# A two-layer transformer block on one core: the sums over channels added on VectorE before one product with ones, and the convolution's steps spread differently over the attention's rounds

## The reference

```python
def rms_norm_2(x, g):                       # over the 1024 channels
    y = xf * lax.rsqrt(jnp.mean(xf * xf, axis=-1, keepdims=True) + NORM_EPS)
    return (y * g).astype(x.dtype)

def layer_norm(x, g, b):
    mu = jnp.mean(xf, axis=-1, keepdims=True)
    xc = xf - mu
    y = xc * lax.rsqrt(jnp.mean(xc * xc, axis=-1, keepdims=True) + NORM_EPS)
    ...
for l in range(DEPTH_2):
    n = rms_norm_2(h, mix_norm_g[l])
    proj = jnp.einsum("btd,de->bte", n, w_in[l])     # q, k, v, indexer, rnn, conv, gates
    attn = dsa_attention(...)                        # top-64 keys per query, 8 heads
    rnn = rg_lru_branch(...)
    cnv = conformer_conv_branch(...)                 # 31-tap depthwise conv, layer_norm, swish
    h = h + (g_attn * attn @ w_o_attn + g_rnn * rnn @ w_o_rnn + g_conv * cnv @ w_o_conv) @ w_out
    f = rms_norm_2(h, ffn_norm_g[l])
    h = h + (silu(f @ w_gate) * (f @ w_up)) @ w_down
return h[:, N_META:]
```

## Time and profile before

| | |
|---|---|
| median of 3 runs | 1950.4 us (1950.38 to 1953.06) |
| profiled execution, its own time | 1948.66 us |
| its span, first to last instruction | 1946.9 us |
| mean granted TensorE clock | 0.996 |
| PE busy | 1885.7 us (97% of the span) |
| PEld busy | 1494.1 us (77%) |
| DVE busy | 735.4 us (38%) |
| ACT busy | 479.4 us (25%) |
| POOL busy | 98.4 us (5%) |
| HBM read | 222.34 MB, 115 GB/s over the span |

### The profile page before, as it was taken

How to read it: one execution, slowest core, us unless ns; L and a number is a source line. 1 busy time by engine, 2 the same in 40 slices (tenths; PEclk the granted TensorE clock), 3 DMA queues, 4 the chain that set the end, 5 groups by cost and what they waited for, 6 DMA issues and landing times.

```text
span 1946.9 us, 31281 instructions
## 1 busy us (share of the span) xinstructions
PE 1885.7 (97%) x13612; PEld 1494.1 (77%) x13612; DVE 735.4 (38%) x1518; ACT 479.4 (25%) x1012; POOL 98.4 (5%) x117
## 2 busy tenths in 40 slices
PE   8999999888889999999999999999999999999999
PEld 3344645888878888788888888887887888888888
DVE  1234426555533876754221000027859442210000
ACT  2112235333334114552202000041135422010000
POOL 0001300323300000000000000000000000000000
PEclk9999999999999999999999999999999999999999
DMA  8311300000043343332333433433433333433442
GB/s 312 140 58 67 114 22 2 4 4 4 4 154 130 130 151 130 130 128 90 120 140 109 156 147 151 143 139 130 152 130 130 130 108 130 151 130 141 162 161 99
DMA packets 33225, 225.41 MB, mean 116 GB/s; under 512 B 4672, under 2 KB 6080, under 8 KB 6336
## 3 DMA queue, kind: packets, MB, share of 16 engines
q1 hardware_dynamic: 33088, 223.40, 32.1%
HBM read 222.34 MB, written 1.05 MB: 115 GB/s over the span
## 4 chain that ended last, share of the span: by engine, by line
PE 89%; DVE 5%; issue 2%; DVEq 1%; ACT 1%; SPq 1%; DMA 0%; POOL 0%; ACTq 0%
PE PS L450 22%; PE PS L596 12%; PE PS L1554 8%; PE PS L615 8%; PE PS L621 8%; PE PS L634 8%; PE PS L1192 2%; PE PS L463 1%; PE PS L1493 1%; PE PS L1194 1%; DVE arena L840 1%; PE PS L1169 1%; PE PS L1645 1%; PE PS L569 1%; DVEq L842 1%
## 5 line engine op out<-in xcount | busy, mean ns | idle before, releaser
L450 PE MATMUL PS<-arena,ring 128*128 128x272 f32 (+1 forms) x2176 | 499.7, 390 | 0.0
L450 PEld LDWEIGHTS PS<-arena,ring 128*128 128x128 f32 x2176 | 413.0, 191 | 77.1 <-issue 1.4
L596 PE MATMUL PS<-arena,ring 128*128 128x272 f32 (+1 forms) x1024 | 229.6, 386 | 2.1 <-DVE arena L1036 2.1
L596 PEld LDWEIGHTS PS<-arena,ring 128*128 128x128 f32 x1024 | 194.5, 190 | 35.8 <-DVE arena L1036 2.9
L840 DVE SCALAR_TENSOR_TENSOR arena<-arena,par 128x272 f32<-128x272 f32 (+1 forms) x480 | 214.9, 489 | 16.3 <-issue 0.4
L615 PE MATMUL PS<-arena,ring 128*128 128x272 f32 (+1 forms) x704 | 163.8, 386 | 0.0
L621 PE MATMUL PS<-arena,ring 128*128 128x272 f32 (+1 forms) x704 | 163.8, 386 | 0.0
L1554 PE MATMUL PS<-arena,ring 128*128 128x512 f32 (+2 forms) x448 | 158.3, 514 | 1.7 <-DVEq L1845 1.7
L634 PE MATMUL PS<-arena,ring 128*128 128x272 f32 (+1 forms) x704 | 157.1, 386 | 1.1 <-issue 1.1
L634 PEld LDWEIGHTS PS<-arena,ring 128*128 128x128 f32 x704 | 133.8, 190 | 24.5 <-issue 1.9
L615 PEld LDWEIGHTS PS<-arena,ring 128*128 128x128 f32 x704 | 133.9, 190 | 22.7
(11 more groups left out here) (327 smaller groups left out, 1918.5 us busy)
## 6 DMA issues: line engine op xcount, KB each, us to landing
ring<-stream_dram SPq DMA_DIRECT2D x207, 1024.0 KB, 4.9
arena<-x_dram SPq DMA_DIRECT2D x1, 2048.0 KB, 11.6
cst<-const_dram SPq DMA_DIRECT2D x1, 1080.0 KB, 7.2
out_dram<-H SPq DMA_DIRECT2D x4, 256.0 KB, 2.2
cst<-const_dram SPq DMA_DIRECT2D x1, 912.0 KB, 17.6
arena<-stream_dram SPq DMA_DIRECT2D x1, 512.0 KB, 7.2
par<-param_dram SPq DMA_DIRECT2D x2, 177.0 KB, 11.0
c<-const_dram SPq DMA_DIRECT2D x1, 128.0 KB, 2.5
```

Source lines behind the costliest of these rows:

```text
L450: last = mm(PS[:, (m + f) % 4, nw], lslot(l, n, KD, 256)[:, k, P * f:P * f + P], NT[:, k, nw], start=k == 0, stop=k == KD - 1)
L596: last = mm(PS[:, i % 4, NQ], lslot(l, n, KD, 256)[:, k, P * (i % 2):P * (i % 2) + P], src[:, k, NQ], start=k == 0, stop=k == KD - 1)
```

## The change

Three things are changed.

1. A sum over channels is made in two parts: VectorE adds the 8 channel groups to one (`add_tiles`, a `tensor_reduce` whose innermost axis is the group, so that it steps 272 elements between reads), and TensorE does one product of `ones` with the result (`sum_parts`). There are 9 such places: 5 in layer 0, 4 in layer 1. New semaphores (`added`, `fn_added`, `conv_sq_in`) carry it, and each place has a new target (`SQF`, `SQS`, `CSUM`).
2. The order around the sums: in layer 0 the mix norm's sum stands behind the second indexer projection in place of the first; the feed-forward norm's sum stands behind the first gate tile in place of the first up tile; VectorE makes `H` behind `MIX` in place of ahead of it, and ScalarE waits for it (`h_made`) before it keeps the projections.
3. `conv_until` has other numbers.

```diff
+        CSUM = TQ[:, 1:3, :]
-            def sum_tiles(src, bank, n, done):
-                for k in range(n):
-                    last = mm(PS[:, bank, NQ], ones, src[:, k, NQ], start=k == 0, stop=k == n - 1)
-                last.then_inc(done, 1)
+            def sum_parts(src, bank, nw, done):
+
+                mm(PS[:, bank, nw], ones, src[:, nw], start=True, stop=True).then_inc(done, 1)

             def norm_sums(nth, bank, nw):

-                for k in range(KD):
-                    pe.wait_ge(L["sq"], B["sq"] + KD * nth + k + 1)
-                    last = mm(PS[:, bank, nw], ones, SQ2[:, k, nw], start=k == 0, stop=k == KD - 1)
-                last.then_inc(L["sums"], 1)
+                pe.wait_ge(L["added"], B["added"] + nth + 1)
+                sum_parts(SQS, bank, nw, L["sums"])
...
                 if m == 0 and l == 0:
-                    pe.wait_ge(fn_sq, KD)
-                    for k in range(KD):
-                        last = mm(PS[:, 4, META:T2], ones, SQ1[:, k, 0:TX], start=k == 0, stop=k == KD - 1)
-                    last.then_inc(fn_sums, 1)
-                if m == 0:
+                    pe.wait_ge(fn_added, 1)
+                    sum_parts(SQF, 4, slice(META, T2), fn_sums)
+                if m == (0 if l else 1):
                     norm_sums(0, 5, NW)
...
                     pe.wait_ge(L["conv_sum_in"], B["conv_sum_in"] + 1)
-                    sum_tiles(CVG, 4, KD, L["conv_sum"])
+                    sum_parts(CSUM[:, 0], 4, NQ, L["conv_sum"])
                 if i == 8:
-                    pe.wait_ge(L["conv_sq"], B["conv_sq"] + 1)
-                    sum_tiles(CSQ, 5, KD, L["conv_sq_sum"])
+                    pe.wait_ge(L["conv_sq_in"], B["conv_sq_in"] + 1)
+                    sum_parts(CSUM[:, 1], 5, NQ, L["conv_sq_sum"])
...
                 last.then_inc(L["gate_made"], 1)
+                if i == 0:
+                    norm_sums(1, 4, NQ)
...
                 last.then_inc(L["up_made"], 1)
-                if i == 0:
-                    norm_sums(1, 4, NQ)
...
                 inverse_root(RS2[:, 0, :], MIX, D, L["root"])
+                act.wait_ge(h_made, 1)
...
+        def add_tiles(v, out, tiles):
+
+            return v.tensor_reduce(out, tiles.rearrange("p k t -> p t k"), axis=AX_X, op=ALU.add)
...
+            if l == 0:
+                dve.wait_ge(fn_sq, KD)
+                add_tiles(v, SQF[:, META:T2], SQ1[:, :, 0:TX]).then_inc(fn_added, 1)
+            dve.wait_ge(L["sq"], B["sq"] + KD)
+            add_tiles(v, SQS, SQ2).then_inc(L["added"], 1)
             dve.wait_ge(L["lam_exp"], B["lam_exp"] + 1)
...
                 dve.wait_ge(fn_root, 1)
-                for k in range(KD):
-                    stt(H[:, k, META:T2], XT[:, k, TX:T1], final_g[:, k:k + 1], RSF[:, META:T2], ALU.mult, ALU.mult)
                 dve.wait_ge(L["sums"], B["sums"] + 1)
...
                 tt(MIX[:, META:T2], MIX[:, META:T2], RSF[:, META:T2], ALU.mult).then_inc(mix_in, 1)
+                for k in range(KD):
+                    last = stt(H[:, k, META:T2], XT[:, k, TX:T1], final_g[:, k:k + 1], RSF[:, META:T2],
+                               ALU.mult, ALU.mult)
+                last.then_inc(h_made, 1)
...
-            conv_until = (68, 90, 94, 96, 98, 98, 106, 124) if len(R) == 6 else (68, 90, 100, 102, 104, 124)
+            conv_until = (68, 80, 86, 90, 92, 94, 106, 124) if len(R) == 6 else (68, 80, 88, 92, 98, 124)
...
-            dve.sem_inc(L["conv_sum_in"], 1)
+            add_tiles(v, CSUM[:, 0, NQ], CVG[:, :, NQ]).then_inc(L["conv_sum_in"], 1)
...
+                if i == 6:
+                    dve.wait_ge(L["conv_sq"], B["conv_sq"] + 1)
+                    add_tiles(v, CSUM[:, 1, NQ], CSQ[:, :, NQ]).then_inc(L["conv_sq_in"], 1)
...
-            dr()
+            dve.wait_ge(L["sq"], B["sq"] + 2 * KD)
+            add_tiles(v, SQS[:, NQ], SQ2[:, :, NQ]).then_inc(L["added"], 1)
             dve.wait_ge(L["root"], B["root"] + 2)
```

More of the change, by code:

```diff
@@ L242, in build @@
         DEC = cut(7024, KD, T2)
-        RSF, MIX, COSR, SINR = (RS2[:, i, :] for i in range(1, 5))
+        RSF, MIX, COSR, SINR, SQS, SQF = (RS2[:, i, :] for i in range(1, 7))
         MG = RG
@@ L279, in build @@
         steps_over, vt_made, vt_kept = sem("steps_over"), sem("vt_made"), sem("vt_kept")
-        zeroed = [sem(f"zeroed{i}") for i in range(60)]
+        zeroed = [sem(f"zeroed{i}") for i in range(64)]
         SCAN_COUNTS = dict(
@@ L357, in build @@
         KSQ, RSK = cut(30136, 2, T2), cut(30680, 2, T2)
-        consts2_in, params2_in, fm_ready, mix_in = sem("consts2_in"), sem("params2_in"), sem("fm_ready"), sem("mix_in")
+        consts2_in, params2_in, fm_ready, fn_added, mix_in, h_made = (
+            sem("consts2_in"), sem("params2_in"), sem("fm_ready"), sem("fn_added"), sem("mix_in"), sem("h_made"))
         out_in = sem("out_in")
         LAYER_COUNTS = dict(
-            made=END_M, kept=END_M, gained=2 * KD, gate_scaled=2, sq=2 * KD, sums=2, root=2, normed=2 * KD, wi_made=1, wi_kept=1, v_turned=3, v_kept=3, iswap=1, iswap2=1, iroped=2, logits=4,
+            made=END_M, kept=END_M, gained=2 * KD, gate_scaled=2, sq=2 * KD, added=2, sums=2, root=2, normed=2 * KD, wi_made=1, wi_kept=1, v_turned=3, v_kept=3, iswap=1, iswap2=1, iroped=2, logits=4,
             relu=4, relu_used=4, u4=1, lam_exp=1, lam_one=1, lam_ln=1, coef=1, decays=1, sq_in=1, b_root=1, rnn_over=1,
             qk_sq=1, qk_sums=3, qk_read=3, qk_root=1, qk_normed=1, swapped=3, swap_used=3, scores=6, max=6, exp=6,
-            prob=6, pt_made=6, pt_kept=6, o_made=8, o_kept=8, conv_sum_in=1, conv_sum=1, conv_cent=1, conv_sq=1,
+            prob=6, pt_made=6, pt_kept=6, o_made=8, o_kept=8, conv_sum_in=1, conv_sum=1, conv_cent=1, conv_sq=1, conv_sq_in=1,
             conv_sq_sum=1, conv_root=1, conv_normed=1, conv_out=1, br_made=32, br_kept=32, merged=1, gate_made=FT,
```

## The result

| | before | changed |
|---|---|---|
| first comparison, median (4 executions each) | 1950.39 us | 1934.95 us |
| lowest to highest | 1949.82 to 1953.06 us | 1932.82 to 1936.72 us |
| profiled execution, its own time | 1948.66 us | 1936.72 us |
| its span and mean granted clock | 1946.9 us, 0.996 | 1934.9 us, 0.992 |

The ratio is 0.9918, with a 95% interval of 0.9901 to 0.9935: faster by 15.4 us, where 28.3 were forecast. The time lies 1 us above the range of 1918.5 to 1934 us.

What follows compares the result with a forecast made beforehand. TensorE, busy 97% of the span, was taken as the bound. Products removed 28.1, less waits 0.5, plus moved steps 1.0, less 0.3, gave 28.3 us off 1950.4: 1922.1 us, own range 1919 to 1926, whole range 1918.5 to 1934.

Steps and rivals of the forecast that it cites:

- The nine additions: On VectorE at the sums over channels: 2.42 or 2.29 us each by element count, leaving TensorE 0.5 us of waits.
- The products removed: TensorE drops seven of eight products in each sum over channels: 3.21 or 3.02 us a sum, 28.1 us together.
- the moved steps: Convolution steps moved between rounds: 1.0 us won at layer 1's first round, 0.3 us lost at its third, nothing in layer 0.
- the first of the three signs of being wrong: For the additions on VectorE: the forecast is wrong if the reduction's time is not that of its element count.
- the rival of the doubled stride: Strided additions take 4.8 and 4.6 us each, so waits at the norms take back 10.1 us: 1932.2 us; chance 22%.
- The 0.3 us at layer 1's third round: The last pair's start between maximum and reciprocal makes scores 0.3 us late for TensorE's transposes.
- The first norms of layer 0: Final and mix norm: 0.1 us of wait at the final norm, none at the mix norm; KI at 607.2 instead of 613.31.
- The weight stream: Rival: in the layers, late weight transfers give back 20 us at most, about half more likely, 1932 us; chance 5%.

Runs made afterwards that it cites:

- tree and later sums: Changed kernel with three two-operand additions per sum, and the feed-forward norms' and layer 1's mix norm's sums one tile later: 1924.2 us plain median.
- e2_in_order: Changed kernel with its nine additions summing 8 neighbouring tokens, so reading in order (sums not the reference's): 1927.1 us median.
- e6_later: Changed kernel with its four waiting sums one TensorE tile later: 1924.86 us median, ratio 0.9851 to the kernel before.
- e8_strides: Changed kernel with extra VectorE reductions and one-input operations at several inner steps, beside layer 1's last down projection; one execution, no reduction over 3.85 us.

## Why the prediction was wrong, point by point

Two terms failed. The nine additions were priced by their element count alone, and the range had nothing for the granted clock, which is not the same in two sets of executions. By the first alone the time would be 1950.4 - 21.9 = 1928.5 us (worked out below), outside the forecast's own 1919 to 1926 and inside the whole range; the clock made up the other 6 us, which carried the median to 1934.95.

**The products removed: right.** 3.21 and 3.02 us a sum, 28.1 us in all. With 0.7 us of the moved steps and 0.3 us of wait, the version that hides the rest of the additions (tree and later sums) should be 28.5 us below the kernel before; it is 27.6 us below at the full clock, and 27 to 28 us in the layers' part.

**The additions: the step that failed.** "I take 2.42 and 2.29, because operations of the same element count cost the same here whatever they compute". For reductions and operations of two operands that read in order it holds (e2_in_order: 2415 and 2283 ns); as a rule for whatever is computed it did not hold even in the trace of before, where a copy of 544 elements takes 445 ns (L901) and an addition of 544 takes 724 (L833). With the stride of 272 elements they take 3819 and 3612 ns, 1.58 times as much: the first of the three signs of being wrong that the forecast had named. So TensorE's waits at the sums are 5.9 and not 0.5 us. Four products behind a wait take 0.7 and not 0.45 us, about 1 us more, which the sum had not. The waits came at the four places where the rival of the doubled stride had put them: at the three where the forecast had 0.1 to 0.2 us, and at layer 1's mix norm, where it had none and 0.15 us to spare. At the other five nothing waits, as forecast. The corrected sum is 28.3 - 5.4 - 1 = 21.9 us; 21.4 us are measured at the full clock, and 21 us in the layers' part.

**The rival of the doubled stride** was right in mechanism and too dear: 10.1 us for twice the duration, 5.4 us for 1.58 times. That its 1932.2 us lies near the median of 1934.95 is the clock's doing, not its price's. The Trainium skill's page "Advanced Engine Details and Errata", section "SBUF Cachelines", which spoke for it, agrees with the runs: the full price comes at a step of 16 bytes. The page "SBUF — State Buffer", in the note on cachelines of its section "Door 1: The DMA port swizzle", adds that one can stride 4 fp32 elements for free. Here a step of 3 elements costs 2.92 and one of 4 costs 3.81 against 2.29 us, so the measurement decides: 2 are free, 4 are not.

**The moved steps: right in the main.** 1.0 us at layer 1's first round, nothing won in layer 0; that ScalarE's decays end the wait there is read from the earlier trace rows and was not tested by itself. Layer 0's wait is 2.8 and not 2.5 us in the profile after, which takes 0.3 us away. The 0.3 us at layer 1's third round did not appear: TensorE has no wait for the scaled scores there. So the net of 0.7 us is right, with its 0.3 us at another place.

**The first norms of layer 0: right but for the addition.** From the first projection to KI it takes 17.3 us against 15.8 forecast and 21.8 before; in e2_in_order 15.9. No wait for `NT` in any version, and for `H` only in e6_later, where its cover was taken away.

**The weight stream:** no wait for a transfer in the layers in any profile of the changed kernel. That rival falls.

**What the forecast put at nothing: the clock.** It was made against an execution with a mean clock of 0.996, and the first comparison set four executions at 0.992 to 0.995 beside it (the clocks of the four of before are not on record). At about 2 us for each 0.001 that is some 5 to 6 us of the 12.9 us that were missing from the median; the slow additions and the restarts are 6.4. The forecast took 3.9 us for what a measurement can tell from no change and had no term for the clock in its range. The same two programs gave ratios of 0.9918, 0.9864 and 0.9884 in three comparisons, and the first two intervals do not meet. What makes the clock fall in one execution and not in the next is open: the program, and what TensorE did ahead of the dip, were the same.

## What to carry to other kernels

Price an access pattern, not only an element count: an fp32 reduction on VectorE that reads at an inner step of 4 elements or more took about 1.6 times as long here as one that reads in order, and a tree of additions over whole tiles (2.6 us) does the same sum sooner than one strided reduction (3.8 us). Such a price can be measured by a few instructions put where the engine is idle, as in e8_strides, before a forecast needs it. When work moves from a busy engine to an idle one, the gain is what is taken away less what is now waited for; put the consumer one tile of the busy engine behind the producer, unless another chain hangs on it, as `H` did here. Where the granted clock wanders between executions, compare more than four of each, and give the clock beside the time.

## What the runs showed of the hardware that I had not expected

The price of the stride has steps: 2.29 us up to 2 elements, 2.92 at 3, 3.81 at 4 and no more than 3.85 beyond, for a reduction of 2048 elements (2040 at steps of 3 and 5). And one program on one chip ran from 1946.6 to 1962.5 us, with a mean clock of 0.998 to 0.990 that falls as the time rises. Over the 13 profiles of all kernels the dips in and ahead of the layers fall in the same few stretches (265 to 280, 320 to 350, 560 to 591, 800 to 850, 900 to 945 and 1480 to 1530 us), the one at 560 in all of them, the others in some and not in others.
